# Eight input tiles in flight at once, weights first, the activation table early, and fifteen matmuls on ones ahead of a two-block transformer kernel

## The reference

```python
def first_block(x, norm1_g, w_in, ...):
    h = rms_norm(x, norm1_g[l])
    proj = h @ w_in[l]
    # cut from proj: q, k, v, fg, conv_in (a, b), pool_in
    ...
    x = x + mix @ w_out[l]
    h2 = rms_norm(x, norm2_g[l])
    ...
    x = x + (silu(gate) * val) @ w_down[l]

def rms_norm(x, g):
    return x * rsqrt(mean(x * x, axis=-1) + EPS) * g
```

## Time and profile before

| | us |
|---|---|
| median of 3 runs | 2931.82 |
| lowest and highest of them | 2931.12, 2937.29 |
| the profiled execution | 2931.09 |
| its span, first to last instruction | 2929.3 |

### The profile page before, as it was taken

The page is one execution under the profiler, slowest core; times in us unless marked ns, Lnnn a source line. Parts: engine busy times, 40 slices in busy tenths (PEclk is TensorE's granted clock), DMA queues, the critical chain, the costliest instruction groups (busy, mean ns, idle before and its releaser), DMA issues.

```text
span 2929.3 us, 31554 instructions
## 1 busy us (share of the span) xinstructions
PE 2858.6 (98%) x13108; PEld 2318.8 (79%) x13108; DVE 1393.8 (48%) x1657; ACT 960.5 (33%) x1265; POOL 367.6 (13%) x328
## 2 busy tenths in 40 slices
PE   8999999999999999999999999999999999999997
PEld 6877668888888888788878888666787888888886
DVE  6776544453535354643234444665655213233335
ACT  4313442321212121321236556654353221111112
POOL 1213112000000000111002222033321000000003
PEclk9999999999999999999999999999999999999999
DMA  3225523111111111245523331674641111111113
GB/s 117 80 79 140 145 63 111 51 40 54 45 56 40 54 36 61 76 144 161 196 73 107 97 97 64 184 217 144 230 139 68 38 58 40 57 37 62 36 62 126
DMA packets 88575, 270.01 MB, mean 92 GB/s; under 512 B 12520, under 2 KB 17256, under 8 KB 88432
## 3 DMA queue, kind: packets, MB, share of 16 engines
q1 hardware_dynamic: 73936, 221.61, 24.3%
q0 software_dynamic: 14496, 46.38, 4.6%
HBM read 215.35 MB, written 52.59 MB: 91 GB/s over the span
## 4 chain that ended last, share of the span: by engine, by line
PE 84%; DVE 7%; ACT 3%; issue 2%; POOL 1%; DMA 1%; SPq 0%; DVEq 0%; POOLq 0%; ACTq 0%
PE ps L213 83%; DVE cacc L184 1%; ACT PB L178 1%; PE ps L216 1%; POOL ga L181 1%; DVE PB L184 1%; DMA xin<-in_xT 1%; DVE ps L193 1%; DVE YA L181 1%; POOL YA L181 0%; DVE AL L184 0%; DVE XT L181 0%; DVE stk L181 0%; DVE XR L181 0%; ACT gt L178 0%
## 5 line engine op out<-in xcount | busy, mean ns | idle before, releaser
L213 PE MATMUL ps<-AH,wh 128*128 128x512 f32 (+1 forms) x2216 | 880.6, 397 | 31.5 <-DVE wl L181 11.7
L213 PE MATMUL ps<-AH,wl 128*128 128x512 f32 (+1 forms) x2216 | 865.2, 390 | 0.0
L213 PE MATMUL ps<-AL,wh 128*128 128x512 f32 (+1 forms) x2216 | 864.8, 390 | 0.0
L181 DVE TENSOR_TENSOR wl<-raw,wh 128x1024 fp32r<-128x1024 f32 (+2 forms) x226 | 271.7, 1202 | 800.0 <-ACT wh L178 799.9
L213 PEld LDWEIGHTS ps<-AH,wh 128*128 128x128 f32 (+1 forms) x2216 | 415.8, 188 | 130.3 <-DVE wl L181 9.4
L178 ACT ACTIVATE wh<-raw 128x1024 fp32r<-128x1024 f32 (+2 forms) x273 | 251.5, 921 | 757.0 <-PE ps L213 749.4
L213 PEld LDWEIGHTS ps<-AH,wl 128*128 128x128 f32 (+1 forms) x2216 | 415.5, 187 | 90.1
L213 PEld LDWEIGHTS ps<-AL,wh 128*128 128x128 f32 (+1 forms) x2216 | 416.1, 188 | 87.8 <-issue 3.0
L213 PE MATMUL ps<-UH,wh 128*128 128x512 f32 (+1 forms) x840 | 325.2, 387 | 0.0
L213 PE MATMUL ps<-UL,wh 128*128 128x512 f32 (+1 forms) x840 | 325.1, 387 | 0.0
L213 PE MATMUL ps<-UH,wl 128*128 128x512 f32 (+1 forms) x840 | 325.1, 387 | 0.0
(11 more groups left out here) (227 smaller groups left out, 3229.4 us busy)
## 6 DMA issues: line engine op xcount, KB each, us to landing
raw<-in_w_up SPq DMA_DIRECT2D x44, 512.0 KB, 3.4
raw<-in_w_gu SPq DMA_DIRECT2D x44, 512.0 KB, 3.4
raw<-in_w_w2in SPq DMA_DIRECT2D x32, 512.0 KB, 4.3
raw<-in_w_down SPq DMA_DIRECT2D x48, 256.0 KB, 2.6
raw<-in_w_down SPq DMA_DIRECT2D x32, 320.0 KB, 2.8
xin<-in_xT SPq DMA_DIRECT2D x16, 512.0 KB, 4.7
stk<-scr_ka SPq DMA_DIRECT2D x32, 256.0 KB, 8.1
raw<-in_w_w2v SPq DMA_DIRECT2D x16, 512.0 KB, 3.5
```

The lines of the kernel that those rows point to most:

```text
L181: return Issued(self, self.e.tensor_tensor(out, a, b, op))
L213: return Issued(self, self.e.matmul(out, l, r, start=start, stop=stop))
```

## The change

It has five parts, all in the first stage.

- SP issues weight tile 0 first, then x tile 0, `vec` and x tiles 1 to 7 without a wait between them, then weight tile 1 and the pool weights. Each x tile has a semaphore that no other transfer in flight uses, but for tile 0, which shares dvec with `vec` (ACT waits for both, 32).
- `cst` goes out last, in five pieces of 26 (the last 24) partitions, behind a wait for ACT's fourth high part. Whoever needs it calls `constants`, which waits for three semaphores.
- ACT begins with a copy of one column, which DVE has set to zero; the compiler puts ACT's table load ahead of it. Then it makes wh of weight tile 0 before AH of x tile 0. DVE follows in the same order.
- PE runs fifteen matmuls of 128x512 on a tile of ones (`stk`, written by POOL at the start of the stage, semaphore kone) into a PSUM bank that is not in use yet, ahead of the first real one.
- The table `LD` of the last stages, which says at what count some semaphores stand, is moved by 16 in three places.

```diff
@@ pe_a
+        ones = self.stk1[0][2]
+        q.wait_ge(S.kone, 1)
+        for _ in range(15):
+            q.mm(self.bank(7), ones[:, 0:128], ones[:, 0:512], True, True)
@@ pe_a, win, ahead of the statistics
-                        q.wait_ge(S.dcst, 16)
+                        self.constants(q)
                         q.wait_ge(S.xacc, 7)
@@ act_a
-        q.wait_ge(S.dvec, 16)
+        q.wait_ge(S.step, 1)
+        q.act(self.small[:, 74:75], self.small[:, 73:74], ACT.Copy)
+        self.w_high(q, 0)
         for k in range(NT):
-            q.wait_ge(self.dld(k % 3), 16 * (k // 3 + 1))
+            if k == 0:
+                q.wait_ge(S.dvec, 32)
+            elif k < 7:
+                q.wait_ge(self.x_sem(k), 16)
+            else:
+                q.wait_ge(S.dcst, 16)
             q.act(self.Ah[k], self.xin[k][:, :], ACT.Copy, scale=self.V("g1", k)).then_inc(S.xh)
-            if k == 0:
-                self.w_high(q, 0)
...
-        q.wait_ge(S.dcst, 16)
+        self.constants(q)
@@ dve_a
+        q.memset(self.small[:, 73:74], 0.0).then_inc(S.step)
+        self.w_low(q, 0)
         for k in range(NT):
             q.wait_ge(S.xh, k + 1)
             q.stt(self.Al[k], self.xin[k][:, :], self.V("g1", k), f32(self.Ah[k]), ALU.mult, ALU.subtract).then_inc(S.xl)
-            if k == 0:
-                self.w_low(q, 0)
@@ sp_a
-        for k in range(NT):
-            if k >= 3:
-                q.wait_ge(S.xh, k - 2)
-            q.dma(self.xin[k][:, :], self.io["xT"][k, :, :]).then_inc(self.dld(k % 3), 16)
-            if k == 0:
-                q.dma(self.vec[:, :], self.io["vec"]).then_inc(S.dvec, 16)
-                self.w_load(q, 0)
-            if k == 3:
-                q.dma(self.cst[:, :], self.io["cst"]).then_inc(S.dcst, 16)
+        self.w_load(q, 0)
+        q.dma(self.xin[0][:, :], self.io["xT"][0, :, :]).then_inc(S.dvec, 16)
+        q.dma(self.vec[:, :], self.io["vec"]).then_inc(S.dvec, 16)
+        for k in range(1, 7):
+            q.dma(self.xin[k][:, :], self.io["xT"][k, :, :]).then_inc(self.x_sem(k), 16)
+        q.dma(self.xin[7][:, :], self.io["xT"][7, :, :]).then_inc(S.dcst, 16)
         self.w_load(q, 1)
         q.dma(self.pwr[:, 0:128], self.io["w_poolw"][0, :, 0:128]).then_inc(S.dsp0, 16)
         q.dma(self.pwr[:, 128:256], self.io["w_poolw"][1, :, 0:128]).then_inc(S.dsp1, 16)
+        q.wait_ge(S.xh, 4)
+        for i in range(5):
+            r = slice(26 * i, min(26 * i + 26, P))
+            q.dma(self.cst[r, :], self.io["cst"][r, :]).then_inc(self.dld(i // 2), 16)
@@ new functions
+    def constants(self, q):
+
+        q.wait_ge(self.S.dld0, 48)
+        q.wait_ge(self.S.dld1, 48)
+        q.wait_ge(self.S.dld2, 32)
+
+    def x_sem(self, k):
+
+        return (self.S.dld0, self.S.dld1, self.S.dld2, self.S.dld3, self.S.dsp2, self.S.dsp3)[k - 1]
```

More of the change, by code:

```diff
@@ L2523, in sp_na @@
         branch(192)
-    LD = [112, 112, 32, 0, 176, 176, 0, 0]
+    LD = [112, 112, 32, 16, 176, 176, 16, 16]
     def load8(self, i):
```

## The result

The changed kernel takes 2929.64 us (median of 20 executions, 2925.77 to 2933.69), the kernel before on the same chip 2933.28 (20 executions, 2927.52 to 2937.64). The ratio is 0.9986 with an interval of 0.998 to 0.9992: 3.6 us won, where 4.9 were forecast. That lies within the 0.2% called no change, and inside the range. Two single executions far off all others, one of the changed kernel at 5389 us and one of no_ones at 11530, are left out of every mean in this text. A mean is given with its standard error behind ±. The profiled execution of the changed kernel took 2930.03 (span 2928.2), that of the kernel before 2931.09 (span 2929.3), so this pair of profiles differs by only 1.1 us. That the pair shows 6 us won in the opening and 1 us at the end is the question of this study.

What follows compares the result with a forecast made beforehand. PE, busy 98% of the span, was taken as the bound. Statistics starting at 30.6 instead of 35.54 save 4.9 us: 2926.2 from the profiled 2931.09, 2926.9 from the median 2931.82; forecast 2926.5, range 2924.5 to 2930.3.

Steps and rivals of the forecast that it cites:

- The bound: Whole kernel: PE is busy 98% of the span, so time is won only where it stands still or runs at half clock.
- First matmul, 9.3: Opening: with weights first and an early table load, the first real matmul starts at 9.3 instead of 9.41, gain 0.1 us.
- Loads without gates: x7 at 17.1: Opening: with SP not waiting, the last x tile lands at 17.1 instead of 21.07, at 339 GB/s plus 0.9 us lag.
- rival B: Opening loads: lagging DMA engines land x7 at 19 to 20, gain only 1.1 to 3.0 us; chance 0.20.
- rival D: Opening loads: at 389 GB/s x7 lands at 16.0, gain 6.0 us, time 2925.1; chance 0.16.
- The squares, x7 + 13.5: Opening: the sum of squares ends 13.5 us after x7 lands, at 30.6, and sets the start of the statistics.
- PE, 29.8, and the wait for sqacc: Before the statistics: PE is ready at 29.8 and waits 0.8 us for the sum of squares, until 30.6.
- The ones, worth 0.7 beside the loads: Opening: fifteen matmuls on ones raise PE's clock before real work, worth 2.2 us alone but 0.7 beside the loads.
- It moves as a block: After the statistics: every later step hangs on one chain, so all of it shifts by the opening's gain, 4.9 us.
- A: Rival, the sum as forecast: 2926.5, or 2927.2 where the clock is low at 9.3; chance 0.50.
- C: Rival at the statistics: the clock falls there after PE's wait, costing 1.7 us (2928.2) or 3.4 (2929.9); chance 0.10.
- E: Rival, slower than before: the full queue gets in its own way, x7 lands at 23.5, time 2933.5; chance 0.04.

Runs made afterwards that it cites:

- no_ones: The changed kernel without the fifteen matmuls on ones: 2928.18 us, ratio 0.9982; repeated, 2927.7 us, ratio 0.9989.
- gated: The changed kernel with SP's waits on ACT's high parts put back before x tiles 3 to 7: 2933.67 us, ratio 1.0001 to the kernel before.
- O: The changed kernel itself, all five parts in: 2929.64 us, ratio 0.9986 to the kernel before; run once more unchanged, 2929.73 us, ratio 0.9987.
- again_before: The kernel before, run and profiled once more without any edit: 2933.62 us, ratio 1.0003.
- before_hold: The kernel before plus 22 unused filler matmuls ahead of PE's 5.7 us wait for T: 2934.07 us, ratio 1.0003 to the kernel before.
- gate5: The changed kernel with SP's waits put back but two tiles looser than in the kernel before: 2929.87 us, ratio 0.9993 to the kernel before.
- early: The changed kernel with eight vec columns and the first quarter of weight tile 0 loaded first, and twelve ones: 2929.91 us, ratio 0.9989 to the kernel before.
- hold_again: The changed kernel plus 22 unused filler matmuls ahead of the wait for T, measured a second time: 2925.89 us, ratio 0.9982 to the kernel before.
- hold: The changed kernel plus 22 unused filler matmuls ahead of PE's wait for T, first measurement: 2924.62 us, ratio 0.9973 to the kernel before.

## Why the prediction was right, and where it wasn't

*The bound.* Right. Without the loads in flight nothing is won: gated, with all else in place, is as slow as before. What was named as hidden or worth nothing (early table, cst in pieces, the moved waits) gained and cost nothing that gated could show (2933.7 ± 0.6).

*First matmul, 9.3.* Right: 9.17. The third transfer landed at 6.53 (6.8 was taken), and 1.16 and 1.30 of ACT and DVE follow.

*Loads without gates: x7 at 17.1.* Too late by 1.6 us: 15.5. The term that failed is the rate, 339 GB/s, taken from a stretch in which the gates held the queue down. The earlier trace rows had 389 at a share of 1.00 and lower rates at shares of 0.85 to 0.98 right after; with the queue never empty, it is 400 to 415. The lag of 3.1 us, of which rival B was made, did not come. The rate was rival D's, above its 389. "HBM Reference", section Specifications, of the Trainium skill gives about 425 GB/s for a core that streams alone and leads to 15.4; the trace comes within 3% of that rate (415) and to 15.5.

*The squares, x7 + 13.5.* Right: 15.48 to 29.10 is 13.6, and on the path that was named. AH of tile 7 starts 0.02 us behind its landing, the second weight tile's high part 0.02 behind that tile's landing (16.88), and the squares follow. Faster loads of these tiles would still win next to nothing, for another reason: PE is at the statistics by itself at 29.0 to 29.2.

*PE, 29.8, and the wait for sqacc.* PE by itself is at 29.0 to 29.2, as the 15.5 made its wait for x7 vanish. The forecast wait of 0.8 ahead of the statistics is 0.22 in the second profile of O and was 0.82 in the second profile of the kernel before.

*The ones, worth 0.7 beside the loads.* The direction was right, the size too small in the opening, for the same reason: with the squares at 29.1 rather than 30.6, PE's slow beginning is what comes last. Measured, the statistics come 1.1 and 1.8 us later without them, 1.1 and 1.35 of it by PE's pace. That the clock rises under the ones and holds over the idle time to 9.17 was right: the first ones start 0.43 us apart, the last three at 7.03, 7.28 and 7.51, and the real ones at the upper level. "TensorE: Matmul & The Clock Gate", section Part 1, of the Trainium skill has it that activity releases the throttle; the fifteen ones agree. Over the whole kernel the 0.7 could not be found.

*"It moves as a block".* This step failed. The waits did move as a block, to 0.01 us at the wait for T. The low stretches of the clock did not: 6.1 us of lead at 100 us became 1.0 at the end, in three steps of 1.3, 1.4 and 1.6 us, each at a fall, and 0.8 that I can't assign. In the second profile of O a wait of 1.94 us behind DVE's RBc takes 1.6 more. The step took it for granted that a shift changes nothing that follows, although showed falls behind 40 us.

So the forecast of 4.9 us came near the measured 3.6 to 3.8 partly by luck. In the pair of profiles for which the sum was made the opening won 6.3, since the loads were faster than the 339 GB/s taken. But the sum started from a profile whose statistics came late, at 35.54; in again_before and before_hold, with the same opening, they came at 33.12 and 33.09. At 100 us the four profiles with O's opening (6.1, 6.0, 5.8, 4.2 on the table's scale, the last two of the filler runs) have a mean lead of 5.0 over the three with that of before (0, -0.8, 2.4). The two errors, the rate too low and a late profile as the base, cancel, and of these 5.0 us about 1.2 are given back later, by the mean of the executions. The forecast time also started from 2931.82, the median of three executions, where 134 have a mean of 2933.3: 1.5 of the 3.1 us between 2926.5 and 2929.64. That the lead of O shrinks at falls, by those amounts, is shown by windows. What decides where a fall comes, and how the low stretch lies to a wait, is not: the runs moved it (no ones, gates, filler) and could not predict it.

*The rivals.* A's mechanism held with D's rate. B did not occur. C occurred in four profiles: one of the kernel before (again_before), gate5, early and hold_again, which has O's opening. It occurred in neither profile of O itself. Where it occurred 3.4 or 6.8 us ran at half speed. E did not occur.

## What to carry to other kernels

Where one core streams its input at the start, put all loads in flight on semaphores of their own before anything else is tried; without that there was no gain here. Then ask when the bound engine would be ready by itself, since it is the bound at once: here PE ended within 0.1 us of the squares. And when a lead is read off in one stage, follow the same instruction through both traces to the end with the clock beside it, and take two profiles of each kernel. Here the lead came back in steps, and a single pair would have said 6 us, or 1 us, where the executions say 4. And a merged row of a timeline can hide a short wait before each of its parts: compare the starts with the landings before an engine is called the pace.

## What the runs showed of the hardware

- The rate of the loads rose with how many were in flight. With the gates of before it was 243 and 305 GB/s (8 to 16 us in gated), with gates two tiles looser 382, with all ten queued 415 and 407.
- The clock fell behind the sixteen one-column matmuls of the statistics where PE had waited 0.5 to 0.8 us ahead of them (again_before 0.82, gate5 0.58, hold_again 0.46). It held in the first profile of before, where PE did not wait there, in the second of O (0.22) and in before_hold (0.27). In early it fell there too, though PE stood still for at most 0.14 us in the 3 us around them; so the wait is not all that decides it.
- Behind the same wait of 5.7 us the lower level cost 1.7 or 3.05 us, as the fall came early or late in it. In hold 22 matmuls that nobody needs, placed ahead of it, cost nothing and kept the clock at 1.00.
- A DVE operation on 64x1024 (RBc, near 1910) took 1.21 us in ten profiles. It took 2.63, 2.71, 2.87 and 2.89 in the four in which an addition on POOL (1.30 us) began 0.24 to 0.50 us behind its start. Where POOL's began 0.51 to 0.86 behind, in four others, DVE's kept its 1.21 and POOL's took 1.50 to 1.85. What decides which of the two takes longer was not tested.
- After the very first table load (0.74 to 2.02) ACT ran its next instruction at 2.03, without a pause between them.
